# Output bias by a plain load and GpSimd additions; convolution taps ahead of weight copies

## What is computed

```python
def rg_lru_block(x, w_in, b_in, conv_w, conv_b, gate_w, gate_b, lam, w_out, b_out):
    u = jnp.einsum("bsd,de->bse", x, w_in) + b_in
    gate_branch, rec = u[..., :LRU_WIDTH], u[..., LRU_WIDTH:]
    rec = causal_depthwise_conv(rec, conv_w, conv_b)          # 4 taps
    ...                                                       # gates r, i from rec
    a = jnp.exp(log_a)
    mult = jnp.sqrt(-jnp.expm1(2.0 * log_a))
    b = mult * (i_gate * rec)
    _, h = lax.associative_scan(_linear_recurrence_combine, (a, b), axis=1)
    y = jax.nn.gelu(gate_branch, approximate=True) * h
    return jnp.einsum("bse,ed->bsd", y, w_out) + b_out
# and around it: h = h + rg_lru_block(rms_norm(h, mix_norm[0]), ...)
```

## Time and profile before

| | |
|---|---|
| median of 3 runs | 850.73 us |
| profiled execution | 850.19 us |
| its span | 848.1 us |
| PE, PE weight load, DVE, ACT, GpSimd busy | 99%, 88%, 68%, 56%, 0% |
| data moved by DMA | 148.16 MB, mean 175 GB/s |

### The profile page before, as it was taken

One profiled execution on the slowest core, in us unless ns is written; L12 is line 12 of the kernel. 1 busy time (PEld: TensorE's weight loads), 2 busy tenths in 40 slices (PEclk: granted clock), 3 DMA queues, 4 the chain that ended last, 5 costly groups with the idle time before them and its releaser, 6 DMA issues.

```text
span 848.1 us, 12860 instructions
## 1 busy us (share of the span) xinstructions
PE 835.4 (99%) x5151; PEld 743.3 (88%) x5151; DVE 575.1 (68%) x831; ACT 471.3 (56%) x670; POOL 2.1 (0%) x6
## 2 busy tenths in 40 slices
PE   8988999999999999999999999999999999999998
PEld 8988878888888899998888888888999999999887
DVE  5877777566544578776766656545757689888763
ACT  6678475444443566565754444535554856567441
POOL 0000000000000000000000000000000000000000
PEclk9999999999999999999999999999999999999999
DMA  7763679665565554443685565555563463444531
GB/s 234 205 207 124 223 234 295 204 187 175 196 199 187 160 178 124 147 149 100 212 254 172 181 193 180 193 182 180 168 195 119 134 198 108 142 150 128 189 131 49
DMA packets 124494, 148.16 MB, mean 175 GB/s; under 512 B 6243, under 2 KB 101268, under 8 KB 124308
## 3 DMA queue, kind: packets, MB, share of 16 engines
q1 hardware_dynamic: 122772, 144.58, 53.8%
q10 hardware_dynamic: 1376, 1.72, 0.6%
q0 software_dynamic: 288, 1.05, 0.6%
HBM read 146.27 MB, written 2.63 MB: 176 GB/s over the span
## 4 chain that ended last, share of the span: by engine, by line
PE 84%; DVE 8%; ACT 4%; DMA 3%; issue 1%; SPq 0%; DVEq 0%; ACTq 0%
PE bank L516 17%; PE bank L518 17%; PE bank L517 17%; PE bank L458 7%; PE bank L459 6%; PE bank L460 6%; DVE wlo L1558 3%; PE bank L888 2%; PE bank L465 1%; PE bank L466 1%; PE bank L467 1%; DMA raw<-in_lru_gate_w 1%; PE bank L680 1%; PE bank L527 1%; ACT whi L1026 1%
## 5 line engine op out<-in xcount | busy, mean ns | idle before, releaser
L1558 DVE TENSOR_TENSOR wlo<-raw,whi 128x1024 fp32r<-128x1024 f32 (+1 forms) x268 | 315.0, 1212 | 103.8 <-ACT whi L1026 102.8
L1026 ACT ACTIVATE whi<-raw 128x1024 fp32r<-128x1024 f32 (+1 forms) x264 | 265.0, 1047 | 184.6 <-PE bank L518 100.7
L458 PE MATMUL bank<-xhi,whi 128*128 128x256 f32 x576 | 165.2, 287 | 0.5 <-DVEq L1688 0.3
L459 PE MATMUL bank<-xlo,whi 128*128 128x256 f32 x576 | 162.9, 283 | 0.0
L460 PE MATMUL bank<-xhi,wlo 128*128 128x256 f32 x576 | 162.9, 283 | 0.0
L516 PE MATMUL bank<-whi,xhi 128*128 128x512 f32 x376 | 148.6, 395 | 1.0 <-DVE a_gt L1874 0.7
L518 PE MATMUL bank<-whi,xlo 128*128 128x512 f32 x376 | 146.7, 390 | 0.0
L517 PE MATMUL bank<-wlo,xhi 128*128 128x512 f32 x376 | 146.5, 390 | 0.0
L458 PEld LDWEIGHTS bank<-xhi,whi 128*128 128x128 f32 x576 | 110.3, 192 | 2.2 <-ACT whi L1026 0.6
L459 PEld LDWEIGHTS bank<-xlo,whi 128*128 128x128 f32 x576 | 110.4, 192 | 0.1
L460 PEld LDWEIGHTS bank<-xhi,wlo 128*128 128x128 f32 x576 | 110.4, 192 | 0.0
(11 more groups left out here) (324 smaller groups left out, 1214.2 us busy)
## 6 DMA issues: line engine op xcount, KB each, us to landing
raw<-in_ffn_w_in SPq DMA_DIRECT2D x176, 256.0 KB, 3.7
raw<-in_w_in SPq DMA_DIRECT2D x48, 512.0 KB, 4.6
raw<-in_ffn_w_out SPq DMA_DIRECT2D x44, 512.0 KB, 4.2
raw<-in_attn_w_qkv SPq DMA_DIRECT2D x24, 512.0 KB, 4.5
raw<-in_lru_w_in SPq DMA_DIRECT2D x14, 512.0 KB, 4.6
raw<-in_lru_w_out SPq DMA_DIRECT2D x8, 512.0 KB, 3.5
raw<-in_attn_w_o SPq DMA_DIRECT2D x8, 512.0 KB, 4.2
raw<-in_w_out SPq DMA_DIRECT2D x8, 512.0 KB, 4.8
```

The source lines that it names most:

```text
L458: nc.tensor.matmul(dst, wh, hi, start=start, stop=False, skip_group_check=shared)
L459: nc.tensor.matmul(dst, wh, lo, start=False, stop=False, skip_group_check=shared)
L1026: nc.scalar.activation(whi[:, c % RING, part], raw[:, c % RAWS, part], ACT.Copy).then_inc(hi_done, 1)
L1558: nc.vector.tensor_tensor(wlo[:, c % RING, part], raw[:, c % RAWS, part], whi[:, c % RING, part].bitcast(F32), ALU.subtract).then_inc(lo_d ...
```

## The change

The bias is loaded plainly into `xg` by SP's queue, right behind the last rec load and ahead of gates_a's, and GpSimd adds it to the two halves of `h` with two additions, once it has landed and rec chunk 0 is done. DVE waits for these additions in place of the loads. In both ACT's and DVE's list the steps of the convolution move ahead of weight splits: last_tap(0) and convolve(0) ahead of split(2), rec_hi(0) and conv_lo(0) ahead of split(3), last_tap(3) ahead of split(6) on ACT; the sigmoid table load moves behind split(3). conv_lo(3) on DVE goes behind the first half of split_alone(7).

```diff
@@ SyncE
             stage("rec", lambda c: w_in[4 + c], 2)
+            sp.wait_ge(sq_dve, 2)
+            sp.dma_start(xg[:, :, :].rearrange("p a n -> p (a n)"),
+                         bass.AP(t["lru_b_out"].tensor, 0, [[0, P], [1, D]])).then_inc(bout_in, 16)
             gates("gates_a", 0)
@@ GpSimd
-                pool.wait_ge(sq_ready, 4)
-                pool.wait_ge(chunk_done, STAGES["rec"][0] + 2 + 5)
+                pool.wait_ge(bout_in, 16)
+                pool.wait_ge(chunk_done, STAGES["rec"][0] + 5)
                 for a in range(2):
-                    nc.gpsimd.dma_start(h[:, a, :], bass.AP(t["lru_b_out"].tensor, 0, [[0, P], [1, D]]),
-                                        accum_op=ALU.add).then_inc(bout_in, 16)
-
+                    nc.gpsimd.tensor_tensor(h[:, a, :], h[:, a, :], whole_bias, ALU.add).then_inc(bias_added, 1)
+
+            whole_bias = xg[:, :, :].rearrange("p a n -> p (a n)")
@@ ScalarE
             nc.scalar.activation(sp_a, sp_a, ACT.Ln, bias=1.0).then_inc(sp_abs, 1)
-            split(2)
...
+            last_tap(0)
+            split(2)
+            rec_hi(0)
+            split(3)
             nc.scalar.preload_act_table_set("sigmoid_and_others")
-            last_tap(0)
-            split(3)
-            rec_hi(0)
             last_tap(1)
...
             rec_hi(2)
+            last_tap(3)
             split(6)
-            last_tap(3)
             gate_sigmoids("gates_a", 0)
@@ VectorE
             split_part(1, 1)
-            split(2)
...
-            def split_alone(c):
+            def split_alone(c, *halves):
 
                 dve.wait_ge(chunk_done, c + 1)
-                for n in range(2):
+                for n in halves or range(2):
...
             convolve(0)
+            split(2)
+            conv_lo(0)
             split(3)
-            conv_lo(0)
             convolve(1)
...
             convolve(3)
             split(6)
+            split_alone(7, 0)
             conv_lo(3)
-            split_alone(7)
+            split_alone(7, 1)
...
-            dve.wait_ge(bout_in, 32)
+            dve.wait_ge(bias_added, 2)
             residual_wide("lru_out", 0)
```

More of the change, by code:

```diff
@@ L278, in build @@
         bias_rows = sem("bias_rows")
+        bias_added = sem("bias_added")
         s_bucket = sem("bucket_in")
```

## The result

The changed kernel takes 844.71 us, the median of 4 runs (844.17 to 845.24), beside 850.44 us for the kernel before in the same comparison. The ratio is 0.9934, with a 95% interval of 0.9917 to 0.9952. The profiled execution has a span of 843.0 us; before it was 848.1.

The account below looks back on a forecast made before the run. PE, busy 99%, bounds the kernel; holes and low clock offered 7.9 us. DVE's lead of 6.1 us less a 1.2 us hold left 4.9 us, from 850.7 to 845.8, with no clock gain at lru_out; range 843.4 to 850.0.

Parts of the forecast that it names:

- signs of being wrong: Listed in advance: a hole ahead of chunk 2 or 3, split(4) waiting for its load, lru_out's hole as long as before.
- The two holes: PE stands 2.50 us ahead of gates_b and 2.19 us ahead of lru_out; with low clock, 7.9 us to be had.
- The new order laid out with old durations: ACT and DVE schedule: convolve(3) at 40.5, a 6.1 us lead on DVE; split(9) 5.6 us earlier, at 55.7.
- the case without hold: DVE not delayed by GpSimd's additions, d = 0: lru_out can start at 73.4, hole 0.8 us.
- The covers: Slack for delayed steps: chunk 2's first half ready 0.9 us before PE wants it; gates_a's later loads cost 0.
- The hold d: Time GpSimd's two bias additions hold up DVE: one of two held at DVE's own length, d = 1.2 us.
- rival (b): Additions exclude DVE whole, each 2.35 us, d = 4.7, lead shrinks to 1.4 us: 849.3; chance 0.15.
- one of the two is held: The choice behind d: of GpSimd's two additions, one delays DVE for its length, 1.2 us.
- The sum: DVE's lead 6.1 - 1.2 = 4.9 us sets split(9); lru_out starts at 74.1, no gain of clock counted there.
- Rival (a): No hold on DVE and full clock at lru_out, hole 0.8 us: 5.6 + 1.5 = 7.1 us, 843.6; chance 0.17.
- Rival (d): gates_b weights late for another reason than the bias; reordering alone carries it, about 847.5, still faster; chance 0.10.
- Rival (c): Slower: hold on DVE longer than its whole lead, d = 9.8 at four operations each, 854.4; chance 0.08.

Follow-up runs that it names:

- order_only: The changed kernel with the old accumulating bias load back, so only the new order of taps and weight copies remains: 845.51 us, ratio 0.9955.
- no_add: The changed kernel without the two GpSimd additions, load and waits kept, output bias left out of the result: 842.57 us, ratio 0.9918.
- the trace with the fill: The changed kernel with eight idle 128x128 matmuls put into PE's wait ahead of lru_out: 844.07 us, ratio 0.9937.

## Why the prediction was right, and where it was off

The forecast was 845.8, the measured time 844.71. The holes, their cause and the new order were as I had them; the hold on DVE was not, and it is luck that this hardly shows in the time. One of my own signs of being wrong came true, a hole ahead of lru_out as long as before: 2.26 us, where I had 1.5.

- **The two holes and the cause of the first.** Right. With the accumulating load the gates_b halves took 8.4 and 10.0 us to land, with the plain load 3.8 and 4.7 us (the two kernels without additions in that stretch, order_only and no_add). The tap behind split(6) made the hole. What made the weights late stays in part open: the change replaces two accumulating loads by one plain one and also issues it 11 us earlier, and no run takes these apart. The low clock behind the second hole reaches into a third window (82 to 84, 0.90), so the windows of before lose 1.7 us there and not 1.5.
- **The new order laid out with old durations.** Right to 0.3 us where nothing interferes. PE reached the end of the stage before lru_out at 72.66, where I had 72.6. For the case without hold I had convolve(3) at 40.5, the second whi copy of chunk 8 at 55.2, split(9) at 55.7, lru_out at 73.4 and a hole of 0.8 us; the kernel without additions shows 40.51, 55.1, 55.9, 73.67 and 0.81.
- **The covers.** gates_a's later issue cost 0.3 to 0.4 us of ACT's time with the plain load (0.6 with the accumulating one) and none of DVE's. Chunk 2 was ready for PE; no hole came ahead of it.
- **The hold d: the term that was mis-sized.** I took 1.2 us, the measured hold is 2.40 - 0.17 = 2.2 us. An addition takes 2.41 us, not DVE's 1.2: the length in rival (b) (2.35). And the bias landed after 4.3 us at 25.3, not at 27.7. It did not matter when it landed, since DVE's copies and conv_lo(0), one right behind the other and all with two SBUF inputs, kept the first addition out until 28.9; then it took its turn, and DVE's next two-input operation, the small edge step, waited for the whole of it. (In the trace with the fill the bias landed at 26.4, and the edge step took 2.40 us just the same.) The second addition ran beside the taps. So "one of the two is held" came true, but by another path: I had an addition meet a weight copy, and took the length from the wrong engine. The mechanism was rival (b)'s, with one addition in place of two.
- **The sum.** Lead on DVE 6.1 - 2.2 = 3.9; measured 4.1 at convolve(3), at split(9) and at lru_out, where the forecast had 4.9. The missing 0.8 us were made up by about 1 us in the feed-forward stretch, which the forecast did not hold: the profiled execution took 845.20 us, where I had 845.3. The median is another 0.5 us lower because two of the four executions kept the clock at lru_out, where I had counted no gain of clock. That the forecast came close is this sum of errors, not a right d.
- **Rival (a)** did not come about in this kernel; its figure, 843.6, is what removing the hold should give: 842.1 to 842.6 measured, 1 to 1.5 us better. Its condition was mis-stated: with DVE's lead at 6.1 and split(9)'s at 5.6, a d above 0.6 and not 0.3 widens the hole past 0.93.
- **Rival (d)**, that the bias is not to blame, is out by the landing times. Rival (c) would have needed additions over 2.5 times as long as DVE's and all held; they are twice as long, and one was held.
- **The parts.** The order alone gives 4.1 us, the bias alone 0.7 us. With the order in place, taking the accumulating load away gives 2.9 us if there are no additions (845.51 to 842.57). Of this 1.9 us are the earlier start of lru_out (75.57 and 73.67), the rest goes with the clock: order_only's one execution at the full clock took 844.55 us. With the additions as the change has them it is about 0.8 us, which the runs don't separate from nothing (ratios 0.9955 and 0.9934 or 0.9944, with overlapping intervals).

## To carry to other kernels

A hole that is closed need not be time that is won: with the bias alone the hole at gates_b went, and came back ahead of lru_out. Ask when the last input of the next waiting stage is ready. And ask of a step that waits for a load what stands behind it on its engine: here one swap brought 2.1 us although the load stayed as late as it was. Work moved to GpSimd is not free because GpSimd is idle: price it by what VectorE does in those microseconds, and release it behind an operation of VectorE that reads PSUM. In this kernel one semaphore for that was worth another 2.0 us (by the ratios) to 2.6 us (by the medians) on top of the 5.7 us of the change.

## What was not expected of the hardware

- GpSimd's addition was held off 3.5 us by two-input operations of VectorE that followed each other without a gap (issued at 25.36, 2.41 us long, ended at 31.30), while in the old order, where it was issued during an operation that reads PSUM, it went first and the engines then alternated. What decides whose turn it is, these rows don't show.
- The length of a hole did not decide whether PE's clock fell. In the profiled execution with the order alone PE stood 2.74 us ahead of lru_out and the clock stayed full; in the changed kernel it stood 2.26 us and the clock fell to the lower level. The same kernel goes both ways: four of nine executions of the changed kernel show a mean clock of 0.998 and are some 1 us longer than the five with 0.999 or 1.000. Holes of 0.81 us left the clock full in both traces that have one. What else decides is open. So compare executions of the same mean clock before a us is put down to anything else.

```profile
PE bank L518 <- DVE a_ylo L1799: 2.7, 1, 2.7
...
76.00:78.00 2.00, 2.00 (x11) 1.00 0.68 253
78.00:80.00 2.00, 2.00 (x11) 1.00 0.77 255
```
